# Layer 0's input product in three contraction parts instead of four, with the modulation products in adjacent pairs

## What is computed

```python
mod = silu(c) @ w_mod + b_mod                      # 2048 -> 6144, one row
shift, scale, gate = split(mod, 3)
h = rms_norm(x, g_pre) * (1 + scale) + shift       # 256 x 2048
proj = h @ w_in                                    # -> 5648 columns; the last 2048 are z
# 3600 columns feed sliding-window attention, spatial gating and gated linear attention
y = concat(y_a, y_b, y_c) * silu(z)
out = y @ w_out
x = x + gate * rms_norm(out, g_post)               # then layer 1, then the second stack
```

## Time and profile before

| | us |
|---|---|
| median of 3 runs (2873.79 to 2877.04) | 2874.58 |
| the profiled execution's span | 2875.8 |
| PE busy | 2805.5 (98%) |
| PE weight loads busy | 2416.4 (84%) |
| DVE busy | 2165.9 (75%) |
| ACT busy | 1518.2 (53%) |

### The profile page before, as it was taken

How to read it: one execution, slowest core, us unless ns; L and a number is a source line. 1 busy time by engine, 2 the same in 40 slices (tenths; PEclk the granted TensorE clock), 3 DMA queues, 4 the chain that set the end, 5 groups by cost and what they waited for, 6 DMA issues and landing times.

```text
span 2875.8 us, 37336 instructions
## 1 busy us (share of the span) xinstructions
PE 2805.5 (98%) x14486; PEld 2416.4 (84%) x14486; DVE 2165.9 (75%) x2815; ACT 1518.2 (53%) x2108; POOL 41.5 (1%) x49
## 2 busy tenths in 40 slices
PE   7998998999999999999999999999999999999998
PEld 5886787898889888888888888898888888888887
DVE  8999998779854667666886678746676668866787
ACT  5445554665546554644554455565546445544554
POOL 0000000000000000000000000000000000000000
PEclk9999999999999999999999999999999999999999
DMA  9996597767645454555665556554545555555564
GB/s 394 375 358 228 191 367 294 276 203 260 241 154 179 157 170 153 176 188 193 199 204 184 189 198 202 187 193 157 170 153 174 188 195 198 204 184 190 197 217 156
DMA packets 173745, 610.87 MB, mean 212 GB/s; under 512 B 19665, under 2 KB 19937, under 8 KB 173057
## 3 DMA queue, kind: packets, MB, share of 16 engines
q1 hardware_dynamic: 170770, 599.38, 60.1%
q0 software_dynamic: 1824, 6.61, 0.8%
q10 hardware_dynamic: 976, 2.51, 0.2%
HBM read 606.30 MB, written 2.11 MB: 212 GB/s over the span
## 4 chain that ended last, share of the span: by engine, by line
PE 85%; DVE 9%; ACT 2%; issue 2%; DMA 1%; POOL 0%; SPq 0%; DVEq 0%; POOLq 0%; ACTq 0%
PE ps L2333 16%; PE ps L2264 16%; PE ps L2267 15%; PE ps L2271 15%; PE ps L2343 8%; DVE w_lo L1410 2%; PE ps L2206 2%; DVE raw L1640 2%; PE ps L2310 1%; PE ps L2312 1%; PE ps L2307 1%; PE ps L2543 1%; PE ps L2316 1%; PE ps L2321 1%; PE ps L2319 1%
## 5 line engine op out<-in xcount | busy, mean ns | idle before, releaser
L1004 ACT ACTIVATE w_hi<-raw 128x1024 fp32r<-128x1024 f32 (+3 forms) x942 | 948.8, 1020 | 993.1 <-PE ps L2271 366.5
L1410 DVE TENSOR_TENSOR w_lo<-raw,w_hi 128x1024 fp32r<-128x1024 f32 (+3 forms) x942 | 1091.1, 1177 | 493.5 <-ACT w_hi L1004 489.5
L2333 PE MATMUL ps<-hT_both,w_hi 128*128 128x512 f32 x2048 | 490.5, 391 | 1.1 <-DVE u L1566 0.9
L2264 PE MATMUL ps<-w_hi,hT_both 128*128 128x512 f32 (+3 forms) x1824 | 477.8, 383 | 11.7 <-DVE proj L1612 7.2
L2271 PE MATMUL ps<-w_hi,hT_both 128*128 128x512 f32 (+3 forms) x1824 | 460.0, 373 | 0.0
L2333 PEld LDWEIGHTS ps<-hT_both,w_hi 128*128 128x128 f32 x2048 | 376.0, 188 | 75.1 <-DVE u L1566 1.3
L2267 PE MATMUL ps<-w_lo,hT_both 128*128 128x512 f32 (+3 forms) x1640 | 415.0, 374 | 0.6 <-DVE w_lo L1410 0.6
L2271 PEld LDWEIGHTS ps<-w_hi,hT_both 128*128 128x128 f32 x1824 | 339.1, 188 | 48.7
L2264 PEld LDWEIGHTS ps<-w_hi,hT_both 128*128 128x128 f32 x1824 | 326.8, 189 | 58.0 <-DVE proj L1612 10.6
L2267 PEld LDWEIGHTS ps<-w_lo,hT_both 128*128 128x128 f32 x1640 | 305.1, 188 | 45.2 <-DVE w_lo L1410 1.6
L2343 PEld LDWEIGHTS ps<-hT_both,w_lo 128*128 128x128 f32 x2048 | 262.8, 191 | 10.2
(11 more groups left out here) (309 smaller groups left out, 2619.5 us busy)
## 6 DMA issues: line engine op xcount, KB each, us to landing
raw<-in_w_up SPq DMA_DIRECT2D x256, 512.0 KB, 3.6
raw<-in_w_down SPq DMA_DIRECT2D x256, 512.0 KB, 3.5
raw<-in_w_modT SPq DMA_DIRECT2D x162, 512.0 KB, 5.9
raw<-in_w_rest SPq DMA_DIRECT2D x80, 456.0 KB, 3.4
raw<-in_w_z SPq DMA_DIRECT2D x56, 512.0 KB, 4.3
raw<-in_w_out SPq DMA_DIRECT2D x51, 512.0 KB, 4.4
raw<-in_w_oa SPq DMA_DIRECT2D x32, 512.0 KB, 3.3
raw_more<-in_w_modT SPq DMA_DIRECT2D x30, 512.0 KB, 6.0
```

What stands on the lines that cost most here:

```text
L1004: act.activation(hi_blocks(L % SPLIT_SLOTS, c, w), blocks(raw_at(G), c, w), ACT.Copy).then_inc(S.hi_ready, 1)
L1410: dve.tensor_tensor(blocks(lo_at(G), c, w), blocks(raw_at(G), c, w), hi_blocks(s, c, w).bitcast(F32), ALU.subtract).then_inc(S.group_read, 1)
L2264: pe.matmul(o, rows(hi, c, t), wh[:, c], start=start and c == 0, stop=False)
L2333: pe.matmul(ps[:, bank(job, i, f)], wh[:, c, f * P:(f + 1) * P], hT_both[:, k0 + c].rearrange("p a n -> p (a n)"), start=k0 + c == 0, stop ...
```

## The change

1. **Three parts.** Layer 0's input product is cut into parts of 4, 6 and 6 chunks (`PORTIONS`): 8 tiles by 2, 3 and 3 groups, so 16, 24 and 24 steps, 64 as before. Matmuls and weight loads are the same. There is one pass of seven additions to `proj` less (14 instead of 21 at L1612), and one computation of columns less. The second part needs the columns of 6 chunks, so 24 modulation products now stand in the 13 first steps of `ina0` (16 before), 24 in `inb0` and 22, of the gate, in `inc0` (14 before in `ind0`): 70 in the 64 steps instead of 62. `z0` has 20 instead of 28.
2. **Pairs.** `pace_pairs` gives the modulation loads two at a time, and `mod_products` does two whose slots are adjacent as one 128x2048 instruction.
3. Leads, waits and POOL's late small loads are moved to the matching steps. The rotation starts after step 12 and 14 of `inc0` of 24, that is 12 and 10 steps from the end of the product instead of 7 and 5.

The core of the diff:

```diff
-QUARTERS = 4
-QC = KC // QUARTERS
+PORTIONS = (((0, 4), (4, 6), (10, 6)), ((0, 4), (4, 4), (8, 4), (12, 4)))
+FIRST_INPUT = ("ina", "inb", "inc")
...
+        def pace_pairs(total, steps):
+            return [2 * n for n in pace(total // 2, steps)]
...
-        parts = [(product(f"in{'abcd'[q]}0", hT, lhs0=q * QC, evac="dve" if q else "act", pinned=True),
-                  pace(16, 13) if q < QUARTERS - 1 else pace(14, 16)) for q in range(QUARTERS)]
-        parts += [(product("z0", hT), [1, 1] + pace(20, 12) + pace(6, 17)),
-                  (product("out0", hT, evac="dve", tail=1), pace(32, 30))]
+        parts = [(product(f"{kind}0", hT, lhs0=k0, evac="dve" if k0 else "act", pinned=True), times)
+                 for kind, (k0, _), times in zip(FIRST_INPUT, PORTIONS[0], (
+                     pace_pairs(24, 13), pace_pairs(24, 21), pace_pairs(22, 24)))]
+        parts += [(product("z0", hT), [2, 0] + pace_pairs(12, 12) + pace_pairs(6, 17)),
+                  (product("out0", hT, evac="dve", tail=1), pace_pairs(32, 30))]
...
-        for q, name in enumerate(("inb0", "inc0", "ind0")):
-            lead(name, *after(name, -2, -1), first=2 * q + 2)
+        for kind, (k0, _) in zip(FIRST_INPUT[1:], PORTIONS[0][1:]):
+            lead(f"{kind}0", *after(f"{kind}0", -3, -2, -1), first=k0 // 2)
...
+            def side_by_side(G):
+                return slots[G + 1] == slots[G] + 1 and slots[G + 1] != RAW_SLOTS
...
+                    if second[3] == G + 1 and side_by_side(G):
+                        mod_pair(*first)
+                    else:
+                        mod_product(*first)
+                        mod_product(*second)
...
-                    walk.upto(jobs["ind0"].L + 9)
+                    walk.upto(last_in.L + 12)
```

More of the change, by code:

```diff
@@ L138, in so_far @@
         return self.n.get(sem.name, 0)
-QUARTERS = 4
-QC = KC // QUARTERS
+PORTIONS = (((0, 4), (4, 6), (10, 6)), ((0, 4), (4, 4), (8, 4), (12, 4)))
+FIRST_INPUT = ("ina", "inb", "inc")
 def weight_products():
-    for q in range(QUARTERS):
-        yield f"in{'abcd'[q]}0", "w_in", 0, q * QC, QC, 0, C_Z, C_Z // 8
+    for kind, (k0, cnt) in zip(FIRST_INPUT, PORTIONS[0]):
+        yield f"{kind}0", "w_in", 0, k0, cnt, 0, C_Z, C_Z // 8
     yield "z0", "w_in", 0, 0, KC, C_Z, D, COLS
@@ L546, in build, with portion_mods, portion_of, portion_ends @@
         hT = (hT_hi, hT_lo)
-        def quarter_mods(l, q):
-            return [(l, part * KC + q * QC + k, h) for k in range(QC) for part in range(2) for h in range(2)]
+        def portion_mods(l, q):
+            k0, cnt = PORTIONS[l][q]
+            return [(l, part * KC + k, h) for k in range(k0, k0 + cnt) for part in range(2) for h in range(2)]
+        def portion_of(l, k):
+            return next(q for q, (k0, cnt) in enumerate(PORTIONS[l]) if k0 <= k < k0 + cnt)
+        def portion_ends(l, block):
+            return any(block == KC + k0 + cnt - 1 for k0, cnt in PORTIONS[l])
         def gate_mods(l):
             return [(l, 2 * KC + k, h) for k in range(KC) for h in range(2)]
-        mods_first = [mod_group(*m) for m in quarter_mods(0, 0)]
-        mods = [m for q in range(1, QUARTERS) for m in quarter_mods(0, q)] + gate_mods(0)
-        mods += [m for q in range(QUARTERS) for m in quarter_mods(1, q)] + gate_mods(1)
+        mods_first = [mod_group(*m) for m in portion_mods(0, 0)]
+        mods = [m for q in range(1, len(PORTIONS[0])) for m in portion_mods(0, q)] + gate_mods(0)
+        mods += [m for q in range(len(PORTIONS[1])) for m in portion_mods(1, q)] + gate_mods(1)
         shapes = {name: shape for name, *shape in weight_products()}
@@ L1064, in split_bank @@
                 if layer is not None:
-                    act.wait_ge(S.hcol_ready, QUARTERS * layer + 2 * b // QC + 1)
+                    act.wait_ge(S.hcol_ready, layer * len(PORTIONS[0]) + portion_of(layer, 2 * b) + 1)
                 u = n(S.lhs_hi) - 1
@@ L1298, in mixers1 @@
                 if l == 0:
-                    d = jobs["ind0"]
+                    d = last_in
                     act.wait_ge(S.dve_evacuated, d.E + 6)
@@ L1654, in mod_pair, with mod_products, portion_columns @@
                                          accum_out=mod_part[:, l, block, 0:1]).then_inc(S.group_read, 2)
-                if KC <= block < 2 * KC and block % QC == QC - 1:
+                if portion_ends(l, block):
                     dve.wait_ge(S.group_read, G + 2)
-                    quarter_columns(l, (block - KC) // QC)
-            def quarter_columns(l, q):
-                two = lambda v: v.rearrange("p (s k) -> p s k", s=2)[:, :, q * QC:(q + 1) * QC]
+                    portion_columns(l, block - KC)
+            def side_by_side(G):
+                return slots[G + 1] == slots[G] + 1 and slots[G + 1] != RAW_SLOTS
+            def mod_products(mods):
+                for first, second in zip(mods[::2], mods[1::2]):
+                    G = first[3]
+                    if second[3] == G + 1 and side_by_side(G):
[3 more added lines that the diff above has]
+                        mod_product(*second)
+            def portion_columns(l, last):
+                k0, cnt = PORTIONS[l][portion_of(l, last)]
+                k = slice(k0, k0 + cnt)
+                two = lambda v: v.rearrange("p (s k) -> p s k", s=2)[:, :, k]
                 m = two(mod[:, l, 0:2 * KC])
@@ L1685, in wide @@
                         evacuate(*ended.pop(0)[0:2])
-                    if prev and prev[0].kind in ("inb", "inc", "ind") and j == 1:
+                    if prev and prev[0].kind in FIRST_INPUT[1:] and j == 1:
                         evacuate(*prev)
                         prev = None
-                    for m in mods_at.get(L, ()):
-                        mod_product(*m)
+                    mod_products(mods_at.get(L, ()))
                     if L == 0:
@@ L2251, in group_product @@
                 if pinned(job, i):
-                    start, stop = start and job.kind == "ina", stop and job.kind == "ind"
+                    start, stop = start and job.kind == FIRST_INPUT[0], stop and job.kind == FIRST_INPUT[-1]
                 terms = [(c, t, ps[:, bank(job, i, t), 0:job.width]) for c in range(cnt) for t in tokens]
```

30 lines of the change are left out of this document (14 added, 16 removed).

## The result

| | before | after |
|---|---|---|
| median of 8 runs each, us | 2875.93 (2873.79 to 2877.04) | 2884.69 (2881.97 to 2885.93) |
| the profiled execution's span | 2875.8 | 2880.1 |
| PE busy | 2805.5 (98%) | 2808.1 (97%) |
| DVE busy | 2165.9 (75%) | 2154.3 (75%) |

The change makes the kernel slower: ratio 1.003, 95% interval 1.0022 to 1.0039, +8.8 us by the medians, against a forecast of +0.4 and a range that ended at 2881.5. The profiled spans lie only 4.3 us apart (5.9 with the second profile of the changed kernel): the time lies about 2 us above the span, so the profiled execution of before was a rather slow one of its kind and that of after the quickest of its eight.

What follows compares the result with a forecast made beforehand. PE was 98% busy over the span, with DMA and PE full in `ina0` and DVE full in `inb0` and `inc0`. The terms 0 + 0.8 - 0.4 = +0.4 gave a median of 2875.0 us, range 2867.5 to 2881.5.

Steps and rivals of the forecast that it cites:

- `ina0`, +10.1: In `ina0`, eight more modulation loads, 4.19 MB at 415 GB/s, delay the start of `inb0` by 10.1 us to 85.6.
- The third lead: Ahead of `inb0`, one more lead (two chunks of `hT_both`) costs DVE 0.69 + 0.54 = 1.2 us.
- the clock rival: In `ina0`, TensorE's granted clock falls at the end of the stage, costing +3 us, 2878 in all; 7%.
- The rest of the input product, -9.4: In `inb0` and `inc0`, full DVE saves 9.4 us: additions 7.0, pairs 1.1, a lead 0.7, columns 0.6.
- the DMA stays the bound: After `ina0`, loads below 378 GB/s keep the DMA the bound: about 8 us slower, 2883; 13%.
- PE can follow, its floor is 201.3: In the input product's rest, PE's 48 groups need 115.7 us against DVE's 119.4, 3.7 to spare; floor 201.3.
- No shift at the start of `z0`: DVE 1.9 us later at the input product's end, hidden by its waits for ACT; PE's shift taken as 0.
- `z0`, +0.8: In `z0` with 20 products instead of 28, one more on the path, pairs slightly less: +0.8 us, bounds -5.5 and +2.
- The shadow of ACT: In `z0`, products behind a score piece are free, as DVE waits there for ACT's exponentials and `w_hi` anyway.
- relief cashed in full: In `z0` and the input product, DVE's relief counts fully: 5.5 and 2 us gained, 2867; 20%.
- Later pairs, -0.4: After `z0`, 32 pairs save 1.9 us of DVE, of which -0.4 us counts, bounds -1.5 and +1.5.
- after 560 us nothing changes: Only the stages of layer 0 and the begin of layer 1 matter; beyond 560 us the kernel stays the same.

Runs made afterwards that it cites:

- second profile of the changed kernel: The changed kernel measured and profiled once more, nothing altered; 2882.85 us, ratio 1.0028 to the kernel before.
- half_products: Changed kernel with the twelve product pairs of `ina0` over 128x1024 instead of 128x2048, same loads; 2883.85 us, ratio 1.003.
- light_three: Changed kernel with half of the sums left out of every pair between the start of `ina0` and `z0`, same loads; 2881.25 us, ratio 1.0018.
- light_four: Twin of the changed kernel with four parts and pairs, half of the sums left out of every pair from `ina0` to `z0`; 2872.26 us, ratio 0.9988.
- shadow: Changed kernel with twelve modulation products of `z0` moved one step earlier, behind the score pieces; 2875.23 us, ratio 1.0001 to the kernel before.
- before_shadow: Kernel before with only `z0`'s 20 products of steps 2 to 13 moved, three behind each score piece, two left unshadowed; 2870.3 us, ratio 0.9982.
- before_pairs: Kernel before, still four parts and 28 products in `z0`, with the pairs and even tables of the change; 2875.93 us, ratio 1.0003.
- single: Changed kernel with every modulation product after the first 16 done singly, same places and order; 2884.46 us, ratio 1.0033.
- before_shadow6: Kernel before with three products in each of `z0`'s six shadowed steps, none between, eight instead of six in the last 17 steps; 2871.97 us, ratio 0.9987.
- four_shadow: Kernel before's four parts with pairs everywhere and up to four products behind a score piece in `z0`; 2874.57 us, ratio 0.9997.
- less_gate: Changed kernel with 14 instead of 22 gate products in the input product's last part and 28 in `z0`; 2880.97 us, ratio 1.0019.

## Why the prediction was wrong, step by step

**`ina0`, +10.1: right.** PE's first group of `inb0` starts at 85.59, forecast 85.6, and `half_products` shows that the transfers set it. The rate was 415 GB/s over the 49.5 us of the stretch. The prediction set against its row the 358 GB/s for a core of the Trainium skill's "DMA: Bandwidth & Descriptors", section on bandwidth. The same section gives about 358 as what each of two cores gets when both stream from one memory domain, and says that its single-core figures, up to 425, were taken with the other core idle. This kernel runs on one core, and its 415 agrees with that; it contradicts only the section's sentence that the memory side binds such transfers at about 358. The third lead went nearly as sized. DVE, 77.12 before, starts its first work of `inb0` at 89.04, that is 11.9 later (forecast 11.3), behind this lead:

```profile
88.19 0.69 DVE L1769 TENSOR_TENSOR hT_both<-hf,hT_both 128x512 fp32r<-128x512 f32 x1 [0.53 <-ACT hT_both L1097]
...
89.04 1.10 DVE L1425 TENSOR_TENSOR w_lo_more<-raw_more,w_hi 128x900 fp32r<-128x900 f32 x1 [0.16 <-ACT w_hi L1019]
```

Two marks of it missed: PE was busy 88% there (43.41 of 49.5), not under 80%, and the clock rival didn't happen, the granted clock was 1.00.

**The rest of the input product, -9.4: the work left as counted, the time not all.** From 77.12 to 205.89 before, from 89.04 to 210.11 after: -7.7. The 46 products, 14 additions and `w_lo`s stand in the trace as counted. The missing 1.7 us are nearly all idle time of DVE, 1.9 us from 89 to 206 (busy 115.1 of 117.0) against 0.3 before (116.7 of 117.0). DVE waits for `w_hi`, and ACT for its loads. From 84 to 212 us ACT's largest waits are

```profile
ACT w_hi L1019 <- DMA raw<-in_w_inb: 28.6, 16, 4.5
ACT w_hi L1019 <- DMA raw<-in_w_inc: 17.9, 10, 3.2
```

and at the end it is the first load of `z0`:

```profile
206.68 1.06 ACT L1019 ACTIVATE w_hi<-raw 128x1024 fp32r<-128x1024 f32 x1 [1.54 <-DMA raw<-in_w_z]
```

That is the rival "the DMA stays the bound" in small: 414 to 416 GB/s in 119 to 140 and 180 to 212, and 318 between them. It asked for a rate under 378 over the whole, which didn't come (383 is the mean of the five rows), and its price of 8 us is not what happened; but with eight loads more in the last part the DMA had no reserve left there. DVE is 4.2 us later at group 65 instead of 1.9. All the same this is not the failing step: `light_three`, with a light DVE and PE busy 99% of the stretch, is no earlier than before either.

**"PE can follow, its floor is 201.3": this step failed.** I took 12 weight loads at 0.20 us for a group, 2.41, and 48 of them. The row of `light_three` gives 0.81 start to start for four matmuls, 2.44 for a group and 117.1 for 48:

```profile
84.83 0.98 PE L2293 MATMUL ps<-w_hi,hT_both 128*128 128x450 f32 x4
85.64 0.98 PE L2296 MATMUL ps<-w_lo,hT_both 128*128 128x450 f32 x4
86.46 0.97 PE L2300 MATMUL ps<-w_hi,hT_both 128*128 128x450 f32 x4
87.27 0.97 PE L2293 MATMUL ps<-w_hi,hT_both 128*128 128x450 f32 x4
```

And PE doesn't only multiply groups. Between them stand the transposes of the leads, and ahead of `z0` three blocks of eight, as here in after (0.79 us of PE by the start of the next group, 206.76 to 207.55):

```profile
206.76 1.03 PE L2233 MATMUL ps<-cst,proj 128*128 128x128 f32 x8
...
207.55 1.05 PE L2291 MATMUL ps<-w_hi,hT_both 128*128 128x450 f32 x4
```

From the first group of `inb0` to the first of `z0` PE needs 123.4 us in `light_three` (84.83 to 208.20) and 123.2 in `light_four` (75.55 to 198.78), where I had 115.7. So the floor of the changed kernel is 85.6 + 123.3 = 208.9, not 201.3; the kernel before, with its `inb0` at 75.54, had its floor at 198.8 and 9.3 us of reserve up to 208.16, in which its DVE could be slow (and its granted clock fall to 0.83 in 190 to 200, where it stayed at 1.00 after). The change spends this reserve on `ina0`, all of it and 0.7 more. After that every wait of PE counts. From 85.59 to 210.86 PE took 125.3 us, 2.0 above the 123.3. Its weight loads waited 6.3 us for `w_lo` in 75 to 212 us (total, times, longest), 4.6 of them from 85 us on, after:

```profile
PEld ps L2294 <- DVE w_lo L1425: 6.3, 9, 1.2
```

Those behind the addition to `proj` are gone as forecast, but PE's first group of `z0` comes at

```profile
210.86 1.17 PE L2291 MATMUL ps<-w_hi,hT_both 128*128 128x512 f32 x4
```

2.7 later than before: 0.7 from the floor, 2.0 from waits above it. I had set PE's 115.7 us beside DVE's 119.4 and found 3.7 to spare. With 123.3 PE is the longer of the two by 3.9, and its floor lies 7.6 us higher than I had it, so relief of DVE could not pay for `ina0`.

**"No shift at the start of `z0`": wrong, as a result.** I let ACT's 2.15 us of waits absorb DVE's 1.9. They did absorb 1.3 of 4.2 (0.6 of 4.8 in the second profile), but ACT's own path (`q1T` from PE's transposes, the gelu, `w_hi`) is as late as PE: `q1T` starts at 207.65 instead of 204.69, and from there ACT has no gap up to the `w_hi` at 211.85 instead of 208.92. Before, `q1T` waited 1.30 us for the transposes; now it starts 0.9 us after they do (0.6 before) and stands right behind the `w_hi` that waited for its load, so some 0.3 of the 3.0 may be the load's. Measured +2.9, in the second profile +4.2.

**`z0`, +0.8: mechanism right, size near, and its bigger use overlooked.** The shadow of ACT is shown from both sides by `shadow` and `before_shadow`, and it speaks against the rival "relief cashed in full", which forecast 2867: DVE is relieved of eight products, and in 236 to 271 its idle time goes from 1.8 to 6.0 us. The steps cost +1.0 from group 67 to 75 (263 us before), where I had +0.8 up to 271. Then come +1.1 up to 79 and +1.2 up to 85, each the size of one product more on the path: +3.3, beyond my bound of +2. The end of `z0` gives 3.3 back, so that it adds nothing in the profile. On PE the late steps lose 1.95 from group 79 to 85 and give back 3.55 from there to 91, 1.6 net; `before_pairs` has the same (1.1 lost, 2.7 back), so the pairs' table of these steps does it, and I had not foreseen it. I used the shadow to argue that relief is worth nothing. The same rows said that a product moved into it is worth 1.1 us.

**Later pairs, -0.4, and "after 560 us nothing changes": the second failed.** `out0` to group 152 gives -0.4. But `z1`, at 655 to 700 us, still has modulation products, and the table of pairs costs +2.0 there. On PE the loss comes in two places, 1.05 us at 650 and 1.04 at 690 (times of before). From group 152 to 214 it is 2.1 to 2.2 in each of the eleven profiles with the even tables (`single` too) and 0.0 in `before_shadow` and `before_shadow6`, which keep the old ones. So it is two products in one step, not the wide instruction. Before, the chain of work from 654 to 698 us was PE alone:

```profile
by line: PE ps L2264 30.3%; PE ps L2267 29.3%; PE ps L2271 27.7%; PE ps L2598 4.0%; PE ps L2587 3.9%; PE ps L2206 2.5%; PE ps L2576 2.4%
```

After, it goes through DVE there (start, us, what):

```profile
687.74 2.30 DVE raw L1667 x2
690.04 2.27 DVE w_lo L1425 x2
692.31 0.60 DVE proj L1988
692.92 0.61 DVE proj L1990
693.57 1.16 PE ps L2625 x8
```

PE's matmul L2625 waits for the mixer's `proj` L1990 on DVE, which stands behind two products instead of one.

**The sum.** +2.9 (4.2), `z0` and `out0` about -0.4 to 0, `z1` and `rest1` +2.1: 4.4 to 6.2 at group 300 and 900, where +0.4 was forecast. That the medians are 7.4 to 8.8 apart isn't explained by the profiles. Open in part is why `four_shadow`, whose PE is 3.6 us ahead of `before_shadow` at group 67, is 4.3 us behind it at the end. On PE the lead is gone by group 74 (263.97 against 263.69). Two things differ there: four products behind a score piece instead of three, which was the rival of its expectation, and the granted clock, 0.86 in 217 to 265 against 0.93 in the same stretch of `before_shadow`. No run separates them. After that it falls 1.0 us behind by group 98, 1.6 by 126 and 3.7 by the end of `z1`. A kernel with four parts, pairs in the input product alone, three products in most shadowed steps and the old tables from `out0` on was not tried; the best that ran is `before_shadow` with 2870.3.

## What to carry to other kernels

Before a stage is made longer to relieve a later one, work out the floor of every engine from the new start, and for the engine that is 98% busy count everything that it issues there (transposes, score products), not only the main product. Put work of an in-order engine where it waits for another engine's in-order queue anyway, and take relief from the steps that have no such shadow; a table of numbers that moved nothing but this gave more than the whole restructuring. And look up where a table ends before calling the rest of the span untouched.

## What the runs showed of the hardware

The transfers of this core stood at nearly the same rate in each stretch that they filled: 415 GB/s in `ina0` before and after, 414 in 119 to 140, 416 in 180 to 212. A product over 128x2048 takes 2.21 us start to start in `inc0` (207.90 to 210.11) against 1.14 for one over 128x1024, so a pair saves 0.07 us. PE took 123.2 and 123.4 us for the same 48 groups, from `inb0` to `z0`, in `light_four` and `light_three`, which start them 9 us apart. And most steps of unchanged code repeat between kernels to 0.1 us (`after` and `less_gate` from group 67 to 91), while the executions of one kernel spread by 2.3 us (`light_four`) to 6.5 (the kernel before, 24 executions).
